# Attention heads written feature by query: values as the loaded operand of the product, reciprocals spread by a product

## The reference, cut to what matters

```
p = softmax(logits)                                     # per head, 128 queries x keys (b: with a sink logit)
o = einsum('bqgrk,bqkgd->bqgrd', p, v)                  # 64 features a head
y_a = einsum('ble,ed->bld', o_a, w_branch_a)            # 512 -> 1024
y_b = einsum('ble,ed->bld', o_b, w_branch_b)
mix = sigmoid(g_a) * y_a + sigmoid(g_b) * y_b
```

## Time and profile before

| | |
|---|---|
| median of 3 runs | 1327.68 us |
| the profiled execution | 1328.05 us |
| its span in the trace | 1325.9 us |
| PE busy in the span | 1249.1 us (94%) |
| PE busy from 95 to 300 us | 202.98 of 205.00 us |
| DVE, ACT, POOL busy from 95 to 300 us | 141.78, 103.84, 67.05 us |

### The profile page before, as it was taken

The page is one execution under the profiler, slowest core; times in us unless marked ns, Lnnn a source line. Parts: engine busy times, 40 slices in busy tenths (PEclk is TensorE's granted clock), DMA queues, the critical chain, the costliest instruction groups (busy, mean ns, idle before and its releaser), DMA issues.

```text
span 1325.9 us, 17097 instructions
## 1 busy us (share of the span) xinstructions
PE 1249.1 (94%) x5986; PEld 921.5 (69%) x5986; DVE 611.8 (46%) x1121; ACT 460.1 (35%) x767; POOL 530.7 (40%) x681
## 2 busy tenths in 40 slices
PE   6999999999999999999999999999999599898794
PEld 4767777778888888888888788777888444333342
DVE  4868768626542422222227765564352442222116
ACT  5657543445444233142245434254223100000002
POOL 4644323235655645545556637336453101111100
PEclk9999999999999999999999999999999789999998
DMA  6422212122343434334333334213339689999984
GB/s 210 112 64 62 66 48 65 49 64 79 95 110 104 135 89 134 96 96 127 96 95 111 95 80 112 64 49 111 93 117 378 224 339 421 424 424 426 425 372 199
DMA packets 210998, 214.23 MB, mean 162 GB/s; under 512 B 31435, under 2 KB 192957, under 8 KB 198260
## 3 DMA queue, kind: packets, MB, share of 16 engines
q1 hardware_dynamic: 201856, 203.14, 45.3%
q0 software_dynamic: 4752, 8.10, 1.7%
q10 hardware_dynamic: 4324, 2.12, 0.5%
HBM read 205.76 MB, written 16.78 MB: 168 GB/s over the span
## 4 chain that ended last, share of the span: by engine, by line
issue 38%; POOL 31%; PE 25%; DVE 3%; ACT 1%; POOLq 0%; DMA 0%; DVEq 0%; ACTq 0%
POOL wlo L595 31%; PE bank L2070 9%; PE bank L2087 5%; PE bank L1717 3%; PE bank L1719 3%; PE bank L1718 3%; PE side L1747 1%; ACT hid L1016 1%; DVE hid L1570 1%; PE side L1719 1%; PE side L1718 1%; PE side L1717 1%; PE bank L2155 1%; PE side L1998 1%; ACT hidT L1019 0%
## 5 line engine op out<-in xcount | busy, mean ns | idle before, releaser
L595 POOL TENSOR_TENSOR wlo<-raw,whi 128x256 fp32r<-128x256 f32 x644 | 497.1, 803 | 526.8 <-ACT whi L699 526.6
L1718 PE MATMUL bank<-actB_lo,whi 128*128 128x512 f32 x608 | 237.0, 390 | 0.0
L1717 PE MATMUL bank<-actB_hi,whi 128*128 128x512 f32 x576 | 227.9, 396 | 0.5 <-POOL wlo L595 0.5
L1719 PE MATMUL bank<-actB_hi,wlo 128*128 128x512 f32 x576 | 224.6, 390 | 0.0
L699 ACT ACTIVATE whi<-raw 128x1024 fp32r<-128x1024 f32 x161 | 169.0, 1051 | 150.3 <-PE bank L1719 124.9
L1717 PE MATMUL bank<-actA_hi,whi 128*128 128x512 f32 x400 | 157.1, 393 | 1.7 <-DVE actA_lo L1099 1.6
L1719 PE MATMUL bank<-actA_hi,wlo 128*128 128x512 f32 x400 | 155.9, 390 | 0.0
L1718 PE MATMUL bank<-actA_lo,whi 128*128 128x512 f32 x400 | 155.9, 390 | 0.0
L1718 PEld LDWEIGHTS bank<-actB_lo,whi 128*128 128x128 f32 x608 | 114.3, 188 | 24.1 <-issue 1.0
L2070 PE MATMUL bank<-gu,xeT 128*64 128x512 f32 x496 | 120.1, 620 | 9.1 <-issue 7.6
L1717 PEld LDWEIGHTS bank<-actB_hi,whi 128*128 128x128 f32 x576 | 108.2, 188 | 25.5 <-issue 2.3
(11 more groups left out here) (379 smaller groups left out, 1622.6 us busy)
## 6 DMA issues: line engine op xcount, KB each, us to landing
gu<-in_w_exp_gate SPq DMA_DIRECT2D x33, 1024.0 KB, 18.4
gu<-in_w_exp_up SPq DMA_DIRECT2D x33, 1024.0 KB, 20.8
dn<-in_w_exp_down SPq DMA_DIRECT2D x33, 1024.0 KB, 23.9
raw<-in_w_in SPq DMA_DIRECT2D x57, 512.0 KB, 3.9
raw<-in_w_up SPq DMA_DIRECT2D x32, 512.0 KB, 3.9
raw<-in_w_down SPq DMA_DIRECT2D x32, 512.0 KB, 3.9
raw<-in_w_out SPq DMA_DIRECT2D x16, 512.0 KB, 4.0
raw<-in_w_in SPq DMA_DIRECT2D x16, 256.0 KB, 3.2
```

Of the source, the lines that this page charges most:

```text
L595: ins = nc.gpsimd.tensor_tensor(wlo[:, slot, at], raw[:, slot, at], whi[:, slot, at].bitcast(F32), ALU.subtract)
L1717: mm(b[:, :], w_hi, hi[:, k, :], start=first, stop=False)
L1718: mm(b[:, :], w_hi, lo[:, k, :], start=False, stop=False)
L1719: ins = mm(b[:, :], w_lo, hi[:, k, :], start=False, stop=last)
```

## The change

- The values' product is turned round: the values of a head (128 keys x 64 features) are loaded, the turned probabilities (128 columns) move. The result is feature by query. The two heads of a pair write the two column halves of the array, that is PSUM partitions 0 to 63 and 64 to 127, and their products alternate.
- The reciprocals must then stand along the queries. A new job ("shares", g), opened in step 4g+7 where the outputs were turned, multiplies a broadcast column of `mx` (64 columns, loaded) with the identity (128 columns, moving): eight products a group.
- DVE copies the shares to `att` and multiplies them by the outputs in `bank[2 + g % 2]`, at the start of step 4g+8 (`heads_out`); ACT's copy to `att` and DVE's product into `o_n` go.
- A pair's heads now lie in one 128-row block of `att`, so the rows of the branch weights are loaded in the same order, as four DMAs of 64 partitions for a chunk where there were two of 128.

```diff
-    for s in range(PAIRS_A + 1):
+    for s in range(STEPS):
         for half in range(2):
             if s < PAIRS_A:
                 jobs.add(("logits", s, half), "dve")
+        if s % GROUP == GROUP - 1 and s >= 2 * GROUP - 1:
+            jobs.add(("shares", s // GROUP - 1), "dve")
         for half in range(2):
-            if s:
+            if 1 <= s < PAIRS_A + 1:
                 jobs.add(("probs_t", s - 1, half), "act")
...
-            return 2 if C_BR <= c < C_OUT or C_BR2 <= c < C_OUT2 or any(q <= c < q + 4 for q in IN1_QUERIES) else 1
+            return 4 if C_BR <= c < C_OUT else 2 if C_BR2 <= c < C_OUT2 or any(q <= c < q + 4 for q in IN1_QUERIES) else 1
...
+            def load_head_branches(first):
+                with sp.Fori(0, NK // RING) as i:
+                    for u in range(RING):
...
+                        sp.wait_ge(lo_made, first + u - RING + 1 + RING * i)
+                        for n in range(2):
+                            for half in range(2):
+                                sp.dma_start(raw[HD * half:HD * (half + 1), slot, n * L:(n + 1) * L]
+                                             .rearrange("d (j n) -> d j n", n=P), br_v[n][half, :, :, at])\
+                                  .then_inc(raw_loaded[slot], 16)
...
-                if s % GROUP == GROUP - 1 and s >= 2 * GROUP - 1:
-                    g = s // GROUP - 1
-                    b, qt = unit(g * GROUP)[:2]
-                    k = 4 if b == "b" else 0
-                    act.wait_ge(S("out_turned"), g + 1)
-                    a(att[:, k:k + 4, qt * P:(qt + 1) * P], bank[2 + g % 2][:, :].rearrange("p (f q) -> p f q", q=P),
-                      ACT.Copy).then_inc(S("att_made"), 1)
...
+            def heads_out(g):
+                b, qt = unit(g * GROUP)[:2]
+                k = 4 if b == "b" else 0
+                dve.wait_ge(S("values_done"), (g + 1) * GROUP)
+                wait_job(dve, ("shares", g))
+                by_block = lambda x: x.rearrange("p (j q) -> p j q", q=P)
+                chain(v.tensor_copy(att[:, k:k + 4, qt * P:(qt + 1) * P], by_block(side_of(("shares", g))[:, :])), freed)
+                chain(v.tensor_tensor(att[:, k:k + 4, qt * P:(qt + 1) * P], att[:, k:k + 4, qt * P:(qt + 1) * P],
+                                      by_block(bank[2 + g % 2][:, :]), ALU.mult), S("att_made"))
...
             for s in range(STEPS):
+                if s % GROUP == 0 and s >= 2 * GROUP:
+                    heads_out(s // GROUP - 2)
...
-                    chain(v.reciprocal(mx[:, g, :], den[:, g, :]))
-                    dve.wait_ge(S("values_done"), (g + 1) * GROUP)
-                    if g >= 2:
-                        dve.wait_ge(S("out_turned"), g - 1)
-                    chain(v.tensor_tensor(o_n[:, g % 2, :].rearrange("p (h d) -> p h d", d=HD),
...
-                          S("outs_made"))
+                    chain(v.reciprocal(mx[:, g, :], den[:, g, :]), S("outs_made"))
                 if SPLIT_STEP <= s < SPLIT_STEP + 4:
                     second_of_branch(4 + s - SPLIT_STEP)
+            heads_out(2 * NT - 1)
...
                     for half in range(2):
-                        h = j + 4 * half
                         wait_freed(pe, ("probs_t", p, half))
-                        for t in range(nk):
-                            ins = mm(bank[2 + g % 2][:, h * HD:(h + 1) * HD], pT[:, half, t * P:(t + 1) * P],
-                                     v_tok[br][:, k0 + t, HD * half:HD * (half + 1)], start=t == 0, stop=t == nk - 1)
+                    for t in range(nk):
+                        for half in range(2):
+                            rows = slice(HD * half, HD * (half + 1))
+                            ins = mm(bank[2 + g % 2][rows, j * P:(j + 1) * P], v_tok[br][:, k0 + t, rows],
+                                     pT[:, half, t * P:(t + 1) * P], start=t == 0, stop=t == nk - 1)
...
-                    for f in range(4):
-                        ins = turn(bank[2 + g % 2][:, f * P:(f + 1) * P], o_n[:, g % 2, f * P:(f + 1) * P])
-                    ins.then_inc(S("out_turned"), 1)
+                    b = open_job(("shares", g))
+                    for j in range(GROUP):
+                        for half in range(2):
+                            h = j + 4 * half
+                            ins = mm(b[HD * half:HD * (half + 1), j * P:(j + 1) * P],
+                                     mx[:, g, h:h + 1].broadcast_to([P, HD]), ident, start=True, stop=True)
+                    close_job(ins)
```

More of the change, by code:

```diff
@@ L274, in gated_blocks @@
         actB_hi, actB_lo, s_at = lay(b_at, ("actB_hi", [P, NK, L], F32R), ("actB_lo", [P, NK, L], F32R))
-        pbuf, pT, o_n, _ = lay(b_at, ("pbuf", [P, 4, L]), ("pT", [P, 2, L]), ("o_n", [P, 2, L]))
+        pbuf, pT, _ = lay(b_at, ("pbuf", [P, 4, L]), ("pT", [P, 2, L]))
         x_tok, gains, x_sq, _ = lay(b_at, ("x_tok", [P, NT, D]), ("gains", [50, P]), ("x_sq", [P, 2, D]))
@@ L364, in gated_blocks @@
         w_in2_v = A["w_in_2"][0].rearrange("(k p) n -> p k n", p=P)
-        br_v = [A[n][0].rearrange("(k p) n -> p k n", p=P) for n in ("w_branch_a", "w_branch_b")]
+        br_v = [A[n][0].rearrange("(half j d) n -> half d j n", half=2, d=HD) for n in ("w_branch_a", "w_branch_b")]
         br2_v = [A[n][0].rearrange("(k p) n -> p k n", p=P) for n in ("w_gla_branch_2", "w_pool_branch_2")]
@@ L441, in load_branches @@
                                    (0, 4, views[0][:, :, at]), (4, 8, views[1][:, :, at]))
+            def load_head_branches(first):
+                with sp.Fori(0, NK // RING) as i:
+                    for u in range(RING):
+                        at = bass.ds(i * (RING * P) + u * P, P)
+                        slot = (first + u) % RING
+                        sp.wait_ge(lo_made, first + u - RING + 1 + RING * i)
[4 more added lines that the diff above has]
+                                  .then_inc(raw_loaded[slot], 16)
             def load_queries(first):
@@ L466, in _ @@
             load_group(17, 16, w_in_v, 2120)
-            load_branches(C_BR, br_v)
+            load_head_branches(C_BR)
             load_group(C_OUT, NK, w_out_v, 0)
@@ L1245, in _ @@
                         chain(v.tensor_tensor(den[:, g, :], den[:, g, :], es[:, g, :], ALU.add))
-                    chain(v.reciprocal(mx[:, g, :], den[:, g, :]))
-                    dve.wait_ge(S("values_done"), (g + 1) * GROUP)
-                    if g >= 2:
-                        dve.wait_ge(S("out_turned"), g - 1)
-                    chain(v.tensor_tensor(o_n[:, g % 2, :].rearrange("p (h d) -> p h d", d=HD),
-                                          bank[2 + g % 2][:, :].rearrange("p (h d) -> p h d", d=HD),
-                                          mx[:, g, :].unsqueeze(2).broadcast_to([P, HEADS, HD]), ALU.mult),
-                          S("outs_made"))
+                    chain(v.reciprocal(mx[:, g, :], den[:, g, :]), S("outs_made"))
                 if SPLIT_STEP <= s < SPLIT_STEP + 4:
                     second_of_branch(4 + s - SPLIT_STEP)
+            heads_out(2 * NT - 1)
             for k in range(4):
```

## The result

The changed kernel takes 1337.27 us, the median of 4 runs (1336.92 to 1337.77), beside 1328.18 for the kernel before in 4 runs (1327.51 to 1330.31). The ratio is 1.0064 with a 95% interval of 1.0051 to 1.0076: slower by 8.5 us (6.8 to 10.1). The forecast was +7.5 us, 1335.2, with 1330.5 to 1339.5 as range. The profiled execution took 1336.92 us with a span of 1335.1, 9.2 more than the span before.

The account below looks back on a forecast made before the run. TensorE's stream was taken to bound the stretch from 95 to 300 us. Values -4.0, shares +5.5, stall +3.7, clock +0.9 and tail +1.4 gave +7.5 us, forecast 1335.2 us, range 1330.5 to 1339.5.

Parts of the forecast that it names:

- values' products, 32 blocks: TensorE's values in pairs on column halves: 14.7 us plus 11.5 for going in and out, against 30.2 before; -4.0 us.
- shares, 7 groups in the stream: On TensorE, eight products replace four transposes per group, +0.79 us each; +5.5 us for 7 groups.
- stall in step 28: TensorE's second logits product waits for VectorE's copy, late behind ScalarE's queue; +3.7 us.
- clock behind it: TensorE, idle in step 28, may then run at half speed; half of 1.7 taken, +0.9 us (0 to 3.4).
- step 8: VectorE's copy would free the shares' bank at 142.44, TensorE arriving at 142.40; next to nothing lost.
- tail: From the last group's shares to the branch projection: 3.2 us instead of 1.81, +1.4 us (1.2 to 1.6).
- clock behind the tail: Half speed after the wait before the branch projection: no term of its own in the sum.
- third rival: Values and shares: column halves run one after the other at 128 columns; +29 us, 1356.9; chance 3 in 100.
- the second: Rival: going in and out of column halves is free for values and shares; -6.9 us, 1320.8; chance 8 in 100.
- first rival: No stall in step 28 because VectorE's copy comes early enough; +2.9 us, 1330.6; chance 9 in 100.

Follow-up runs that it names:

- e3: Changed kernel with the values' products put back as before on the full array, attention layout wrong: 1342.89 us, 5.2 more than the changed kernel.
- e2: Changed kernel with TensorE's shares products directly behind the values' products, no dense products between: 1335.57 us, 2.3 less than the changed kernel.
- e1: Changed kernel with VectorE's copy and product of group 5 in step 27, ahead of branch b's second part: 1331.51 us, 6.2 less.
- e7: Changed kernel with ScalarE making branch b's first part ahead of the chunk's split in step 27: 1335.72 us, 1.6 less.
- e4: Changed kernel with the first third of each step's dense products moved behind the values, so values directly follow logits: 1331.14 us, 6.5 less.
- after: The changed kernel itself, without any follow-up edit: 1337.27 us, ratio 1.0064 to the kernel before.
- e5: Changed kernel with the last group's shares made in step 34 instead of 35, VectorE's copy and product early in 35: 1337.79 us.
- b1: Kernel before the change with its last group's four transposes in step 34 instead of 35: 1328.84 us, ratio 1.0001.
- e6: Changed kernel with the edits of e1, e2, e4 and e5 together: 1325.48 us, ratio 0.9971 to the kernel before.

## Why the prediction was right

All differences between the profiled executions, in us:

| step of the prediction | forecast | trace | how shown |
|---|---|---|---|
| values' products, 32 blocks | -4.0 | -4.3 | e3: +5.2 when undone |
| shares, 7 groups in the stream | +5.5 | +5.2 | trace alone; its passages by e2 |
| stall in step 28 | +3.7 | +3.5 | e1, e7 |
| clock behind it | +0.9 | +1.5 | e1, with the stall |
| step 8 | 0 | +0.15 | trace |
| tail | +1.4 | +1.4 | trace |
| clock behind the tail | none | +1.6 | trace |
| sum | +7.5 | +9.1 | spans: +9.2 |

Up to the projection the terms make 7.5 and the trace has 7.6 behind a start that was 0.5 later; that 0.5 is given back about 965 us further on, among late stretches at half clock that lie differently in the two executions.

Values: by size of block the trace has +0.12, -0.10, -0.33 and -0.57 for 4, 8, 12 and 16 instructions; there are 8, 16, 4 and 4 such blocks, and the weighted sum is -4.3. The pairs run side by side at 0.108, so the third rival falls, and the passage costs 0.36, so the second falls: it would have needed 0.17. e2 shows that the 0.36 hangs on the change of the array's division and not on the products themselves, since it goes where two blocks of one division meet. The Trainium skill (TensorEngine Tiling (Array Packing), Tiling Modes) says that changing the mode drains the engine; e2 and e4 agree, with 0.31 saved by leaving one passage out, and 0.21 by going from one division to another without full products between. Its advice to swap the sides (Performance Considerations) holds here from 8 instructions a block.

Shares: 0.10 in, 1.02 from first product to the turning, and 0.06 in the turning's first gap are 1.18, against 0.44 for the four transposes: 0.74 a group instead of 0.79.

The stall came by the chain that the prediction read from the rows of before: first part, second part, copy, product. It is 0.2 shorter than forecast, because VectorE is free 0.76 us after it starts the second part and not 0.97, a case that the forecast's lower bound of 3.4 had in it. The first rival is out; e1 shows what it would have given, 1331.5 us for a forecast of 1330.6.

The clock is the one term that was mis-sized: +0.9 was taken, half of one stretch, and the trace has +3.1. It shows the whole of one stretch, 3.4 us at 0.50, and another of 3.4 us behind the tail's wait. The term's upper bound, two such stretches, had allowed for it. The prediction had worked out the tail's idle time (3.2 us less the block's own) and had read from the earlier trace rows that 2.40 us of idling can be followed by half speed, and did not put the two together in its sum. That the forecast still lies so near the measured time owes something to luck: how much half clock follows the same wait differed between the kernels here, from 3.4 to 10.2 us, and no row stood behind taking half of one stretch. With both stretches at their full 1.7 it would have said +10.0 for a measured 8.5 (6.8 to 10.1).

## What to carry to other kernels

Putting more operands side by side in the array saves per instruction and costs per block: set the saving of one block against the price of going into and out of the division (here 0.36 us, as much as three pairs of products), and put blocks of one division together before counting on it. When a change lets a second engine free what the first one needs next, look for the one place where that engine stands behind a wait of its own; here moving one step in its order gave back 6.2 us of 8.5. A new wait of TensorE of 2 us or more in an otherwise full stream is to be priced with the clock behind it (1.5 us for a stretch of 3.4 here), and as a range, since its length varied.

## What the runs showed of the hardware

The same wait of TensorE, 2.4 us in step 28, came with 3.4 us at half clock in after and e2, with 6.8 in e4 and e5, and with 10.2 in e3. The two executions with the short stretch are those in which the clock fell 1.1 to 1.3 us after PE had begun again (after: 260.01 and 261.3; e2: 258.59 and 259.7); in the three with a longer one it fell while PE still waited, 0.5 to 0.7 us before it began again (e4: 254.8 and 255.36; e5: 259.6 and 260.32; e3: 260.7 and 261.43). Five executions are no proof. Waits of 2.1 us at the tail were followed by 3.4 us (after, e1, e2, e4, e7) or by none (e3), waits of 1.2 to 1.4 us (before, b1, e5, e6, e7) by none. What decides stays open.

A change of the array's division has three prices here: full to column halves and back 0.36 us, row halves to column halves about 0.2 in place of the 0.4 of a way out and one in, and column halves to column halves on other operands nothing.
